# A decoder layer in fp32 on one core: projections and cross-attention run as one sequence of 48 units

## The reference

```python
m = rmsnorm(mem, g_mem)
k = jnp.einsum('bmd,de->bme', m, w_k)          # prompt: 256 memory tokens, 4 heads of 512
v = jnp.einsum('bmd,de->bme', m, w_v)
def cross_attention(h, mem_k, mem_v, w_q, w_o):
    q = jnp.einsum('btd,de->bte', h, w_q)
    s = jnp.einsum('bthd,bmhd->bhtm', q, mem_k) * (512 ** -0.5)
    p = jax.nn.softmax(s, axis=-1)
    o = jnp.einsum('bhtm,bmhd->bthd', p, mem_v)
    return jnp.einsum('btd,de->bte', o, w_o)
```

## Time and profile before

| what | value |
|---|---|
| median of 3 runs | 2031.25 us (2029.52 to 2032.12) |
| the profiled execution's own time | 2029.23 us |
| its span, first to last instruction | 2027.5 us |
| TensorE busy | 1868.7 us (92%) |
| VectorE busy | 1158.9 us (57%) |
| ScalarE busy | 763.5 us (38%) |
| granted TensorE clock, mean | 0.969 |
| DMA, mean over the span | 179 GB/s |

### The profile page before, as it was taken

How to read it: one execution, slowest core, us unless ns; L and a number is a source line. 1 busy time by engine, 2 the same in 40 slices (tenths; PEclk the granted TensorE clock), 3 DMA queues, 4 the chain that set the end, 5 groups by cost and what they waited for, 6 DMA issues and landing times.

```text
span 2027.5 us, 34488 instructions
## 1 busy us (share of the span) xinstructions
PE 1868.7 (92%) x13799; PEld 1749.6 (86%) x13799; DVE 1158.9 (57%) x1590; ACT 763.5 (38%) x768; POOL 243.3 (12%) x225
## 2 busy tenths in 40 slices
PE   4999999858695999999988999999999999999996
PEld 3999999755694989977764898999999999999996
DVE  5788445473834655555556565666544466665444
ACT  1454554322224343333333234444333344443332
POOL 6000000001711540000000351000000000000331
PEclk9999999889897999999999999999999999999998
DMA  5455555700032545677867366898745789895552
GB/s 158 153 179 166 168 169 186 225 3 11 1 94 84 180 152 168 227 265 265 319 211 274 96 184 184 256 253 238 197 143 172 207 234 246 242 252 148 171 175 95
DMA packets 407132, 362.42 MB, mean 179 GB/s; under 512 B 10975, under 2 KB 373470, under 8 KB 404214
## 3 DMA queue, kind: packets, MB, share of 16 engines
q1 hardware_dynamic: 379686, 336.53, 53.9%
q10 hardware_dynamic: 27392, 25.17, 3.9%
HBM read 345.67 MB, written 16.19 MB: 178 GB/s over the span
## 4 chain that ended last, share of the span: by engine, by line
PE 84%; DVE 8%; issue 3%; ACT 2%; POOL 1%; DMA 1%; DVEq 0%; POOLq 0%; ACTq 0%; SPq 0%
PE ps L419 64%; PE ps L439 9%; PE ps L831 2%; DVE w_lo L403 2%; PE ps L1158 1%; PE ps L1148 1%; PE ps L947 1%; DMA vc<-in_cache_mem_v_dram 1%; PE ps L1047 1%; PE ps L1112 1%; ACT w_hi L396 1%; PE ps L999 1%; DVE cacc L519 0%; DVE Tm L1853 0%; DMA raw<-in_ffn_w_up_dram 0%
## 5 line engine op out<-in xcount | busy, mean ns | idle before, releaser
L396 ACT ACTIVATE w_hi<-raw 128x2048 fp32r<-128x2048 f32 (+1 forms) x289 | 519.9, 1799 | 924.9 <-PE ps L419 784.4
L403 DVE TENSOR_TENSOR w_lo<-raw,w_hi 128x2048 fp32r<-128x2048 f32 (+1 forms) x289 | 629.6, 2179 | 273.4 <-ACT w_hi L396 269.3
L419 PE MATMUL ps<-act_hi,w_lo 128*128 128x264 f32 x2576 | 740.0, 287 | 3.6 <-DVE w_lo L403 1.9
L419 PE MATMUL ps<-act_lo,w_hi 128*128 128x264 f32 x2576 | 732.3, 284 | 0.0
L419 PE MATMUL ps<-act_hi,w_hi 128*128 128x264 f32 x2576 | 731.8, 284 | 0.0
L419 PEld LDWEIGHTS ps<-act_hi,w_lo 128*128 128x128 f32 x2576 | 487.9, 189 | 6.9 <-DVE w_lo L403 6.2
L419 PEld LDWEIGHTS ps<-act_lo,w_hi 128*128 128x128 f32 x2576 | 488.2, 190 | 0.7
L419 PEld LDWEIGHTS ps<-act_hi,w_hi 128*128 128x128 f32 x2576 | 485.5, 188 | 0.0
L419 PE MATMUL ps<-ff_hi,w_lo 128*128 128x264 f32 x704 | 202.0, 287 | 4.3 <-DVE ff_lo L542 4.3
L419 PE MATMUL ps<-ff_hi,w_hi 128*128 128x264 f32 x704 | 201.4, 286 | 0.0
L419 PE MATMUL ps<-ff_lo,w_hi 128*128 128x264 f32 x704 | 200.9, 285 | 0.0
(11 more groups left out here) (365 smaller groups left out, 1944.2 us busy)
## 6 DMA issues: line engine op xcount, KB each, us to landing
raw<-in_w_in_dram SPq DMA_DIRECT2D x56, 1024.0 KB, 6.8
raw<-in_ffn_w_gate_dram SPq DMA_DIRECT2D x44, 1024.0 KB, 5.8
raw<-in_ffn_w_up_dram SPq DMA_DIRECT2D x44, 1024.0 KB, 10.5
raw<-in_ffn_w_down_dram SPq DMA_DIRECT2D x32, 768.0 KB, 4.8
raw<-in_ffn_w_down_dram SPq DMA_DIRECT2D x32, 640.0 KB, 6.1
raw<-in_w_out_dram SPq DMA_DIRECT2D x16, 1024.0 KB, 6.7
raw<-in_xa_w_q_dram SPq DMA_DIRECT2D x16, 1024.0 KB, 6.7
raw<-in_xa_w_k_dram SPq DMA_DIRECT2D x16, 1024.0 KB, 6.3
```

What stands on the lines that cost most here:

```text
L396: act.activation(w_part(ph, w_hi[b]), raw_part(ph, r, half), ACT.Copy)\
L403: dve.tensor_tensor(w_part(ph, w_lo[b]), raw_part(ph, r, half), w_part(ph, w_hi[b]), ALU.subtract)\
L419: mm = pe.matmul(ps[:, acc(ph, u), 0:ph.cols], w[b][:, k, :], v[:, kk + k, 0:ph.cols], start=first and k == 0 and m == 0, stop=last and k ...
```

## The change

The query projection, the two memory projections and most of the attention become one list of 48 units, numbered 0 to 47 on all engines (`unit_at`). The cached keys come by head and then by sample; the first is used after unit 5 instead of after the first unit of `mem_k`. The first 14 key pieces use space in `kT` (three buffers), all others a ring of eight 512 KB buffers. The cached values come as 32 pieces of 512 KB through the same ring, instead of eight loads of 2 MB in two buffers. The queries of the samples are turned head by head, after units 4, 10, 18 and 26. The prompt's keys are turned after units 20, 24, 28, 32, its scores made after 22, 26, 30, 34 and its shares turned after 23, 27, 31, 35. The samples' softmax sits at units 37 to 39, and the first 16 sample values follow units 40 to 47, two each. The rest, 16 sample values and the 16 tiles of prompt values, come after unit 47. The loops of `x_q` are written out. `ring_landed` takes the place of `kc_landed` and `vc_landed`, and the copy of scores with its semaphore `s_kept` is gone. The core of the diff:

```diff
+EARLY = 3
+EARLY_PIECES = 14
+RING = 8
+PIECES = 2 * NB * XH
...
+        mt = [kT[:, 14 + b, :].rearrange("p (c d) -> p c d", c=2) for b in range(2)]
+        early = [kT[:, 4 * b:4 * b + 4, :].rearrange("p (m k) n -> p m (k n)", m=2) for b in range(EARLY)]
+        ring = [place(f"ring{b}", [P, 2, XD], F32, A0 + 4096 * b) for b in range(RING)]
...
+        def piece_at(p):
+
+            if p < EARLY_PIECES:
+                return early[p % EARLY], ring_landed[RING - 1 - p % EARLY], 16 * (p // EARLY + 1)
+            n = p - EARLY_PIECES
+            used = len(range(RING - 1 - n % RING, EARLY_PIECES, EARLY)) if n % RING >= RING - EARLY else 0
+            return ring[n % RING], ring_landed[n % RING], 16 * (used + n // RING + 1)
+
+        def unit_at(m):
+
+            ph = PH[("x_q", "mem_k", "mem_v", "x_o")[m // KT]]
+            return ph, m % KT // 4, m % 4
+
...
+            def load_slot(s):
+
+                ph, i, u = unit_at(2 * s)
+                load(sp, ph, i, u // 2)
+
+            def piece_in(p):
+
+                if p < EARLY_PIECES:
+                    if p >= EARLY:
+                        W(sp, "s_dot", p - EARLY + 1 + 2)
+                elif p < EARLY_PIECES + RING:
+
+                    sp.wait_ge(units_done, PH["mem_k"].u0 + UNIT_CREDIT)
+                elif p < NB * XH + RING:
+                    W(sp, "s_dot", p - RING + 1 + 2)
+                else:
+                    W(sp, "s_o", p - RING - NB * XH + 1)
+                dst, landed, _ = piece_at(p)
+                n = p % (NB * XH)
+                if p < NB * XH:
+                    part = a["cache_mem_k"][0][n % NB, :, n // NB, :]
+                else:
+                    part = a["cache_mem_v"][0][n // XH, :, n % XH, :]
+                sp.dma_start(dst[:, :, :], part.rearrange("(m p) d -> p m d", p=P)).then_inc(landed, 16)
...
+            for s in range(3):
+                load_slot(s)
+            sp.wait_ge(rstd_ready, 2)
+            for p in range(EARLY):
+                piece_in(p)
+            nxt = EARLY
+            for m in range(3 * KT):
+                if m % 2 == 1 and m < 46:
+                    load_slot((m + 5) // 2)
+                if m >= 20 and m % 4 == 0:
+                    rows_out((m - 20) // 4)
+                if 5 <= m < KT and nxt < EARLY_PIECES or KT <= m < 37 or m >= 40:
+                    piece_in(nxt)
+                    nxt += 1
+                    if m >= 40 or 22 <= m <= 30 and m % 2 == 0:
+                        piece_in(nxt)
+                        nxt += 1
+            for p in range(nxt, PIECES):
+                piece_in(p)
+            rows_out(7)
...
+            pool.memset(q_rows[:, :, :].bitcast(F32), 0.0).then_inc(columns_ready, 1)
...
+            def turn_query(h):
+
+                pe.wait_ge(q_halved, h + 1 + 1)
+                if h:
+                    W(pe, "s_dot", (10, 18, 26)[h - 1] - 6 + 1 + 2)
+                for d in range(4):
+                    mm = turn(ps[0:2 * NB, 6, d * P:(d + 1) * P], q_both[:, h, d, :, :].rearrange("p m b -> p (m b)"))
+                mm.then_inc(q_turned, 1)
+
+            def spread_query(n):
+
+                W(pe, "s_dot", n + 1)
+                if n in (0, 6, 14, 22):
+
+                    pe.wait_ge(q_kept, (0, 6, 14, 22).index(n) + 1)
+                h, b = n // NB, n % NB
+                mm = pe.matmul(ps[:, 6 + n % 2, :], pick_row[:, b:b + 1].broadcast_to([P, P]), q_rows[:, h % 2, :],
+                               start=True, stop=True)
+                mm.then_inc(N["s_qb"], 1)
...
+            def sample_values(n):
+
+                b, h = n // XH, n % XH
+                pe.wait_ge(v_mixed, n + 1)
+                at = NB * XH - 1 - (NB * h + b)
+                pe.matmul(ps[0:NB * XH, 6, :], window[:, at:at + NB * XH], piece_at(NB * XH + n)[0][:, 0, :],
+                          start=n == 0, stop=n == NB * XH - 1).then_inc(N["s_o"], 1)
+
+            def prompt_values(j):
+
+                if j >= 2:
+                    W(pe, "att_oe", j - 1)
+                for m in range(2):
+                    mm = pe.matmul(ps[:, 4 + j % 2, 0:T], vm[:, m, j * P:(j + 1) * P],
+                                   prT[:, j // 4, m * T:(m + 1) * T], start=m == 0, stop=m == 1)
+                mm.then_inc(N["att_o"], 1)
+
+            for n in range(3 * KT):
+                ph, i, u = unit_at(n)
+                if n < KT:
+
+                    pe.wait_ge(m_taken, n + 1)
+                    pe.wait_ge(mt_ready, n + 1)
                     for c in range(2):
                         mm = turn(ps[:, W4 + u % 2, c * P:(c + 1) * P], mt[u % 2][:, c, :])
                     mm.then_inc(N["m_turned"], 1)
                     products(pe, ph, i, u, act_hi, act_lo)
...
+                    if n == KT:
+                        pe.wait_ge(m_taken, KT + 2)
+                    wide_products(pe, ph, i, u)
+                if n in (4, 10, 18, 26):
+                    turn_query((4, 10, 18, 26).index(n))
+                if 5 <= n < 5 + NB * XH:
+                    spread_query(n - 5)
+                if n in (20, 24, 28, 32):
+                    turn_keys((n - 20) // 4)
+                if n in (22, 26, 30, 34):
+                    scores((n - 22) // 4)
+                if n in (23, 27, 31, 35):
+                    turn_prompt((n - 23) // 4)
+                if n == 37:
+                    turn_sample_scores()
+                if n == 38:
+                    turn_sample_shares()
+                if n == 40:
+                    pe.wait_ge(columns_ready, 4)
+                if n >= 40:
+                    for v in range(2):
+                        sample_values(2 * (n - 40) + v)
+            for v in range(2):
+                sample_values(16 + v)
+            W(pe, "att_pT", XH)
             rows_wait(pe, 1, 3)
```

The tail on TensorE, and ScalarE's and VectorE's lists:

```diff
-                    mm.then_inc(N["att_o"], 1)
-                sample_values(b)
+            for j in range(KT):
+                prompt_values(j)
+                if j < 14:
+                    sample_values(18 + j)
             pe.wait_ge(rows_copied, 3)
             for d in range(4):
-                mm = turn(ps[:, 4, d * 32:(d + 1) * 32], orow[:, d * P:(d + 1) * P])
+                mm = turn(ps[:, 7, d * 32:(d + 1) * 32], orow[:, d * P:(d + 1) * P])
...
+            def first_values(n):
+
+                dst, landed, count = piece_at(NB * XH + n)
+                act.wait_ge(landed, count)
+                act.activation(dst[:, 0, :], dst[:, 0, :], ACT.Copy, scale=pT_s[:, 0, n:n + 1]).then_inc(v_first, 1)
...
+            for n in range(3 * KT):
+                split(*unit_at(n + 2))
+                if n in (4, 10, 18, 26):
+                    h = (4, 10, 18, 26).index(n)
...
+                    act.activation(q_rows[0:2 * NB, h % 2, :], ps[0:2 * NB, 6, :], ACT.Copy).then_inc(q_kept, 1)
+                if n in (20, 24, 28, 32):
+                    keep_columns((n - 20) // 4)
+                if n >= KT and n % 4 == 3:
+                    keep_rows(n % KT // 4, n // (2 * KT))
+                if n in (22, 26, 30, 34):
+                    exponentials((n - 22) // 4)
+                if n in (23, 27, 31, 35):
+                    h = (n - 23) // 4
+                    W(act, "att_pturned", h + 1)
+                    act.activation(prT[:, h, 0:2 * T], ps[:, 5, :], ACT.Copy).then_inc(N["att_pT"], 1)
...
+                if n >= 39:
+                    for v in range(2):
+                        first_values(2 * (n - 39) + v)
+            for v in range(18, NB * XH):
+                first_values(v)
+            W(act, "s_o", NB * XH)
+            act.activation(orow[:, :], ps[0:NB * XH, 6, :], ACT.Copy).then_inc(rows_copied, 1)
...
+            def halve_query(h):
+
+                dve.wait_ge(acc_free, PH["x_q"].t0 + 4 * h + 4 + ACC_CREDIT)
+                of_samples = q[:, 4 * h:4 * h + 4, T:TT]
+                link(dve.tensor_copy(q_hi[:, h, :, 0, :], of_samples))
+                dve.tensor_tensor(q_both[:, h, :, 1, :], of_samples, q_hi[:, h, :, 0, :], ALU.subtract).then_inc(q_halved, 1)
...
+            def second_values(n):
...
+                dve.wait_ge(v_first, n + 1)
+                v = piece_at(NB * XH + n)[0]
+                dve.scalar_tensor_tensor(out=v[:, 0, :], in0=v[:, 1, :], scalar=pT_s[:, 1, n:n + 1], in1=v[:, 0, :],
+                                         op0=ALU.mult, op1=ALU.add).then_inc(v_mixed, 1)
...
+            for n in range(3 * KT):
+                if n < KT:
+                    query_and_memory(*unit_at(n))
+                    if n % 4 == 3:
+                        halve_query(n // 4)
+                if n in (23, 27, 31, 35):
+                    prompt_shares((n - 23) // 4)
+                if 5 <= n < 5 + NB * XH:
+                    sample_scores(n - 5)
...
+                split(*unit_at(n + 2))
+                if n in (22, 26, 30, 34):
+                    prompt_max((n - 22) // 4)
...
+                if n >= 39:
+                    if n == 39:
```

(46 more changed lines are left out.)

205 lines of the change are left out of this document (53 added, 152 removed).

## The result

The changed kernel takes 2008.2 us (median of 4 runs, 2007.27 to 2009.26) against 2030.38 us (2028.88 to 2032.12) for the kernel before in the same comparison: ratio 0.9891, 95% interval 0.9873 to 0.9908. That is 22.2 us less.

A forecast was written before the change was run, and what follows sets the result against it. TensorE was taken as the bound, with time won only from its idle and slow-clock stretches. Of the attention's 83.8 us, 32.2 + 37.3 + 2.5 = 72.0 us go back: 11.8 us less, 2019.5 us, range 2013 to 2027 us.

The forecast's parts named there:

- what goes back before unit 47 ends: TensorE work moved in among the 48 units (scores, turns, sample values, spreads, gaps, clearing): 32.2 us put back.
- 32 query spreads as before: Spreads of the samples' queries among the units: same 0.43 us each; only the last, now lying inside, adds 0.4 us.
- the 2.5 us for the clock: After unit 47: one drop of TensorE's clock at the tail's 3.2 us gap, 2.5 us; ends 0 and 4.3 us.
- The wait after unit 47: TensorE idles from 1.8 to 5.0 us after unit 47 for sample values 16 and 17: 3.2 us.
- VectorE's work in the `x_q` units: Sample scores in query units, twice 0.69 us on VectorE, fit into its 1.43 us wait for `w_hi`: costed at nothing.
- the signs named: Signs of being right: units 5 to 15 about 6.5 us, unit 47 ending near 1074 us, `x_o` starting near 1114 us.
- Tail rounds: After unit 47: 14 rounds of a prompt tile and a sample value, 1.89 us each, 26.5 us.
- The 1.4 us for inserted gaps: Pieces inserted between units cost 0 to 0.2 us beyond themselves at each of 37 places; 1.4 us taken.
- VectorE paces the tail: Rival 1, after unit 47: slow hand-overs make rounds 2.3 us, costing 5.7 us; 2025 us, chance 0.15.
- gaps cost 0.28 us each: Rival 2, between units: 37 inserted pieces each take 0.28 us of refill, 10.4 us instead of 1.4; 2028.5 us, chance 0.06.
- Keys that land late, the fourth: Rival 4, in `x_q` units: key pieces from 14 on land late and TensorE waits at its spread; folded into rival 2.
- The low clock over the whole tail: Rival 3, after unit 47: tail at clock 0.50 takes 32 us more; 2049 us, chance 0.09 with any other slower case.

The follow-up runs named there:

- the kernel with narrow spreads: The changed kernel with its query spread back at 32 rows instead of 128: 2018.92 us, ratio 0.994 to the kernel before.
- the one with 64 columns: The changed kernel with the sample values' one-hot window 64 columns wide instead of 32, in a new place: 2008.43 us, ratio 0.9892 to the kernel before.
- 64 rows: The changed kernel with its query spread over 64 rows instead of 128: 2019.16 us, ratio 0.9947 to the kernel before.
- 128 columns: The changed kernel with the sample values' one-hot window 128 columns wide instead of 32: 2002.82 us, ratio 0.987 to the kernel before.

## Why the prediction came out wrong

**The step that failed.** It is in what goes back before unit 47 ends: "32 query spreads as before ... There the price is the same 0.43 us". The spread was costed from the earlier trace rows as if unchanged, while the change widens it from 32 to 128 rows. It costs 0.23 us and leaves the next unit at 5.58 us. Measured alone, the wider spread is worth 300.15 - 288.81 = 11.3 us of the units in the old order and 332.42 - 320.87 = 11.5 us in the new one, some 0.36 us a spread. The 0.2 us between 5.78 and 5.58 us was in the prediction as a possible cost of inserting anything; it is a cost of inserting another shape. The plain turns have the full shape, 128x128, and so the unit after them took 5.58 us before as well. The bounds of that term, 0 and 0.2 us at each place, left out that what was there already could get cheaper. With the 11.5 us the forecast would have been 23.3 us less, against 22.2 measured.

**What held.** The new order itself: 11.8 us forecast, 12.4 us of the stage, 11.0 us in the medians. Units 0 to 47 ended within 0.1 us of the sum once the spread is set back to 32 rows. In the tail the near agreement, 39.15 us against 37.3 + 2.5 = 39.8, is partly luck: the rounds took 2.1 us more than forecast, and the 2.5 us for the clock did not come in that execution. The wait after unit 47 was 3.2 us as worked out from ScalarE's and VectorE's lists. TensorE's idle time, 14.5 us before, was 40.65 - 36.02 = 4.6 us in the tail and 0.3 us ahead of it. VectorE's work in the `x_q` units was covered: TensorE was busy for 102.15 of 102.22 us. DMA was not the pace: in this stage TensorE waited for VectorE alone. Of the signs named, `x_q` units with a spread took 6.25 us, not 6.5, unit 47 ended at 1062.15 us, not near 1074, and `x_o` began at 1102.80 us, not near 1114, mostly for the one reason above; with the narrow spread they were 6.6, 1072.51 and 1111.66 us.

**What was off and small.** Tail rounds took 2.04 us, not 1.89: the prediction added up a tile and a value as each runs among its own kind, but they alternate and differ in width, and a prompt tile costs 1.06 us beside a sample value and a value 0.98 us beside a tile, against 0.86 each at one shape. 14 rounds make 2.1 us. The drop of the clock was priced at 2.5 us and cost 3.40 - 1.90 = 1.5 us where it came, against the same pair at 1.00 in the kernel with narrow spreads. In the profiled executions it came in two of the five kernels whose idle gap of 3.2 to 3.3 us was left in place (the changed one and the one with 64 columns) and in none of the other three (32 rows, 64 rows, 128 columns), so it is a term with odds, not a certainty. Of the terms ahead of unit 47 the chain of the kernel with narrow spreads shows the scores at 3.65 us each, as forecast, 4 query turns at 0.44 us, as forecast, and the seven pairs of values at 1.83 us, 12.8 us in all against 12.5. The 1.4 us for inserted gaps is what is left over of the sum, 332.42 against 332.35 us, and was not measured by itself.

**The rivals.** That VectorE paces the tail did not happen, but the thin margin was real: as soon as a round was under 1.8 us it showed, at 0.18 us every other round. That gaps cost 0.28 us each, a price that stood in no row, was refuted; with equal shapes a unit takes 5.58 us after a spread or a score, as it did after plain turns. Keys that land late, the fourth, did not appear either. The low clock over the whole tail did not appear in any run. No rival lay on the side where the result fell.

## What to carry to other kernels

Between full matmuls, the selecting matmul of this kernel was cheaper at 128 rows, and the summing one at 128 columns, padded with zeros, than at the size they need, wherever TensorE was the pace; 64 was no better than 32. It is worth trying for other small matmuls; the turns below show that not every one pays. When reading a diff, compare the shape of every operation that stays, not only the operations that move. And a step whose cost you bound from a row (5.78 against 5.58 us) deserves the question what differs between the two rows, since the answer can turn a cost into a gain.

## What the runs showed of the hardware that I had not expected

A matmul of 32 or 64 rows between matmuls of 128 costs 0.2 us on its own side (0.42 against 0.23 us) and again on what comes next: 0.2 us if that is a unit or a score, 0.15 us if it is a group of turns (0.37 against 0.22 us for two); of 32 or 64 columns, in fp32 and with 512 columns moving, 0.06 us a piece in a pair and 0.2 us for the unit after it. That wider weights take longer to load (0.19 against 0.11 us a load) did not show: the pair became shorter all the same, and the weight load stood idle for 0.24 us after it instead of 0.84. Turns with 16 columns of weights, made at 0.11 us each, show no such price in the changed kernel (0.44 us for four, then a spread at 0.23 and a unit at 5.57 us); no run here tells why, and it stays open. It also stays open what decides whether the clock drops in a gap of 3.2 us: the same gap did it in two traces and not in three. A gap of 2.2 us is no clearer: it was followed by a drop before and not in the old order with a wide spread, where four records of prompt values took 1.10 us after it.
